# Values of a recurrence projected with tokens on the partitions and shifted through memory and GpSimd, in place of a transpose on TensorE

## The reference, cut to what matters

```python
def rwkv_branch(cur, prev, state0, g, mix, ...):      # prev: the row of the token before
    xs = cur + (prev - cur) * mix                     # token shift
    r, k, v, wd, ad = jnp.split(xs, [512, 1024, 1536, 1600], axis=-1)
    ...
    def step(S, inp):
        sa = jnp.einsum('bhij,bhj->bhi', S, -kk_t)
        S = (S * w_t[:, :, None, :] + sa[..., None] * (kk_t * a_t)[:, :, None, :]
             + v_t[..., None] * k_t[:, :, None, :])
        y = jnp.einsum('bhij,bhj->bhi', S, r_t)
```

## Time and profile before

| | |
|---|---|
| median of 3 runs | 1786.79 us (1780.75 to 1791.63) |
| the profiled execution's own time | 1780.9 us |
| its span | 1779.1 us |
| mean granted clock of TensorE | 0.986 |
| TensorE busy | 1704.3 us, 96% of the span, 21338 matmuls |
| VectorE, ScalarE, GpSimd busy | 827.6, 798.0, 417.3 us |
| token-shift projection | about 554 to 858 us of the span |
| recurrence with gates | about 861 to 1570 us |

### The profile page before, as it was taken

How to read it: one execution, slowest core, us unless ns; L and a number is a source line. 1 busy time by engine, 2 the same in 40 slices (tenths; PEclk the granted TensorE clock), 3 DMA queues, 4 the chain that set the end, 5 groups by cost and what they waited for, 6 DMA issues and landing times. The chain is left out here.

```text
span 1779.1 us, 48548 instructions
## 1 busy us (share of the span) xinstructions
PE 1704.3 (96%) x21338; PEld 1397.0 (79%) x21338; DVE 827.6 (47%) x1198; ACT 798.0 (45%) x1656; POOL 417.3 (23%) x282
## 2 busy tenths in 40 slices
PE   6989999999999999999889999999999999889999
PEld 5768888888887888999667777777777777667787
DVE  4334545445445411223445665565655566643332
ACT  5546665666655322223434444444444444313420
POOL 3322212212210000000214454334444333310000
PEclk9999999999999999999889999999999999989999
DMA  6543353344234412214312112112112113466652
GB/s 227 100 90 64 56 51 69 56 57 80 50 109 173 139 74 86 85 55 151 113 45 66 57 52 79 55 52 71 52 51 78 55 52 120 129 246 232 205 171 92
DMA packets 119139, 170.88 MB, mean 96 GB/s; under 512 B 39569, under 2 KB 78993, under 8 KB 118673
## 3 DMA queue, kind: packets, MB, share of 16 engines
q1 hardware_dynamic: 109568, 153.29, 31.6%
q10 hardware_dynamic: 9360, 14.49, 2.2%
HBM read 113.21 MB, written 55.06 MB: 95 GB/s over the span
## 5 line engine op out<-in xcount | busy, mean ns | idle before, releaser
L653 PE MATMUL a_ps_proj<-a_w_hi,a_x_hi 128*128 128x512 f32 x384 | 156.9, 409 | 0.0
L653 PE MATMUL a_ps_proj<-a_w_hi,a_x_lo 128*128 128x512 f32 x384 | 150.9, 393 | 0.0
L653 PE MATMUL a_ps_proj<-a_w_lo,a_x_hi 128*128 128x512 f32 x384 | 150.6, 392 | 0.0
L1057 DVE SCALAR_TENSOR_TENSOR j_out<-j_ps,j_rest,j_part 128x512 f32<-128x512 f32 (+2 forms) x65 | 41.9, 644 | 213.4 <-ACT j_last_cols L1005 163.3
L563 DVE SCALAR_TENSOR_TENSOR a_stage<-a_ps_s,a_new_bias 128x256 f32<-128x256 f32 x64 | 27.1, 424 | 238.6 <-PE a_ps_s L680 238.6
L2222 PE MATMUL r_ps_gate<-gate_w_hi,gate_x_hi 128*128 128x512 f32 x272 | 115.6, 425 | 4.5 <-PEq L66 3.4
L2222 PE MATMUL r_ps_gate<-gate_w_lo,gate_x_hi 128*128 128x512 f32 x272 | 116.3, 428 | 0.0
L2222 PE MATMUL r_ps_gate<-gate_w_hi,gate_x_lo 128*128 128x512 f32 x272 | 116.2, 427 | 0.0
L1003 ACT ACTIVATE j_part<-j_last_cols,j_shift_in 128x1 f32<-128x1 f32 x65 | 19.2, 295 | 205.8 <-PE j_ps L1082 205.7
L1862 DVE TENSOR_TENSOR r_w_mat<-r_ps_w,consts 128x512 f32<-128x512 f32 x83 | 57.3, 690 | 109.3 <-PE r_ps_w L2106 109.2
L338 POOL TENSOR_TENSOR a_xT<-a_xT,a_row 128x1024 f32<-128x1024 f32 x17 | 40.8, 2402 | 253.2 <-DMA a_row<-scratch_rstd 242.2
(11 more groups left out here) (383 smaller groups left out, 4677.6 us busy)
## 6 DMA issues: line engine op xcount, KB each, us to landing
a_xT<-in_x_T SPq DMA_DIRECT2D x17, 512.0 KB, 3.5
scratch_xT<-a_xT SPq DMA_DIRECT2D x17, 512.0 KB, 2.6
raw<-scratch_xT SPq DMA_DIRECT2D x17, 512.0 KB, 4.0
scratch_gates<-r_gate_out SPq DMA_DIRECT2D x34, 256.0 KB, 2.4
z_gate<-scratch_gates SPq DMA_DIRECT2D x17, 512.0 KB, 4.2
xs<-scratch_xs_T SPq DMA_DIRECT2D x15, 576.0 KB, 4.4
a_x<-in_x_prompt SPq DMA_DIRECT2D x16, 512.0 KB, 12.3
scratch_xs_T<-j_out ACTq DMA_DIRECT2D x39, 192.0 KB, 1.9
```

The source lines that it names most:

```text
L653: mm = nc.tensor.matmul(ps_proj[:], a[n % 2][:, k, :], w[:, k, g * AW:(g + 1) * AW], start=(k == 0 and i == 0), stop=(k == KT - 1 and i == 2))
L1057: last = nc.vector.scalar_tensor_tensor(out=out[j][:, 0:n], in0=ps[j][:, 0:n], scalar=rest[:, c:c + 1], in1=part[j][:, 0:n], op0=ALU.mult, ...
```

## The change

The four v blocks leave the blocks of the projection. In their place come value units, one per tile: x is the stationary operand, the four blocks of v weights (512 columns) the moving one, so the result has tokens on the partitions. The two kinds of unit are listed in `SHIFT_UNITS`: in group 0 all nine blocks and then four values, in the others block and value in turn, then the remaining blocks. The parity of a unit's place in the list chooses its bank and buffers.

The token shift of a value tile goes through memory: ScalarE copies PSUM to `part[j]`, SP stores it to `v_raw`, then loads the same rows one token earlier into `v_prev`, and GpSimd computes `(v_prev - part) * v_share + part` into `out[j]`. SP stores that to `v_tok` in four DMAs, 64 tokens and one half of the heads each. TensorE waits for ScalarE's copy alone behind a value unit. ScalarE may write `part[j]` behind a value unit when GpSimd is done with it; VectorE may write `out[j]` when all earlier stores of that parity have landed. The weights are split in another order (`W_ORDER`, `AHEAD`), two blocks a unit at the end. The last rows of v become an output of their own.

In the recurrence the turning, its two jobs and its two ScalarE copies go; SP loads `v_tok` once whole and once with its halves exchanged.

```diff
+SIZES = (4, 4, 3, 3, 3)
+XS_BLOCKS, V_BLOCKS = (0, 1, 2, 3, 4, 5, 6, 7, 12), (8, 9, 10, 11)
+def shift_units():
+    units = []
+    for g, n in enumerate(SIZES):
+        blocks, values = [(g, c, None) for c in range(XS_TILES)], [(g, None, a) for a in range(n)]
+        if g == 0:
+            units += blocks + values
+        else:
+            for i in range(n):
+                units += [blocks[i], values[i]]
+            units += blocks[n:]
+    return units
+def shift_stores(j, before):
+    return sum((1 if a is None else 4) for q, (g, c, a) in enumerate(SHIFT_UNITS[:before]) if q % 2 == j)
...
+        AHEAD = [[m + 2] for m in range(5)] + [[7, 8], [9, 10], [11, 12]]
+        def part_free(eng, q):
+            if q > 1:
+                if SHIFT_UNITS[q - 2][1] is None:
+                    eng.wait_ge(v_mixed, values(q - 2) + 1)
+                else:
+                    eng.wait_ge(mixed[q % 2], mixes(q - 2) + 1)
...
+            def turn_rows(t, j, i):
+                sp.wait_ge(parted[j], i + 1)
+                sp.dma_start(v_rows(t, 0), part[j][:, 0:AW]).then_inc(v_raw_stored, 16)
+                wait(sp, v_mixed, t)
+                sp.wait_ge(v_set_up, 32)
+                sp.wait_ge(v_raw_stored, 16 * (t + 1))
+                sp.dma_start(v_prev[:], v_rows(t, 1)).then_inc(v_prev_loaded, 16)
+            def store_v(t, j):
+                sp.wait_ge(v_mixed, t + 1)
+                for n in range(2):
+                    tokens = slice(n * CH, (n + 1) * CH)
+                    rows = out[j][tokens, 0:AW].rearrange("l (c g d) -> l c g d", g=2, d=HD)
+                    for g in range(2):
+                        sp.dma_start(io["v_tok"][t, g * CH:(g + 1) * CH, n * PAIRS * HD:(n + 1) * PAIRS * HD].rearrange("l (c d) -> l c d", d=HD),
+                                     rows[:, :, g, :]).then_inc(stored[j], 16)
...
+                    if a is not None:
+                        t = tile_of(g, a)
+                        turn_rows(t, j, i)
+                        if last is not None:
+                            store_v(t - 1, last)
+                        last = j
+                        if a == tiles_of(g) - 1:
+                            store_v(t, j)
...
+                pool.wait_ge(v_prev_loaded, 16 * (t + 1))
+                pool.wait_ge(parted[j], q // 2 + 1)
+                nc.gpsimd.tensor_tensor(v_prev[:], v_prev[:], part[j][:, 0:AW], ALU.subtract).then_inc(v_less, 1)
+                pool.wait_ge(v_less, t + 1)
+                nc.gpsimd.tensor_tensor(v_prev[:], v_prev[:], v_share[:], ALU.mult).then_inc(v_shared, 1)
+                pool.wait_ge(v_shared, t + 1)
+                wait(pool, stored[j], 16 * shift_stores(j, q))
+                nc.gpsimd.tensor_tensor(out[j][:, 0:AW], v_prev[:], part[j][:, 0:AW], ALU.add).then_inc(v_mixed, 1)
...
+                    part_free(act, q)
+                    if a is not None:
+                        nc.scalar.activation(part[j][:, 0:AW], ps[j][:], ACT.Copy).then_inc(parted[j], 1)
...
-                    wait(dve, stored[j], 16 * i)
+                        wait(dve, stored[j], 16 * shift_stores(j, q))
...
-                    wait(pe, mixed[j], i)
+                    if q > 1:
+                        if SHIFT_UNITS[q - 2][1] is None:
+                            pe.wait_ge(parted[j], i)
+                        else:
+                            pe.wait_ge(mixed[j], mixes(q - 2) + 1)
...
+                                x, w = ((x_hi, v_w_hi), (x_hi, v_w_lo), (x_lo, v_w_hi))[e]
+                                mm = nc.tensor.matmul(ps[j][:].rearrange("p (c n) -> p c n", c=len(V_BLOCKS)), x[g % 2][:, k, a, :], w[:, :, k, :],
+                                                      start=(k == 0 and e == 0), stop=(k == KT - 1 and e == 2))
...
-        JOB_ORDER = ((("bonus", -1), ("decay", 0), ("k_tok", -1), ("B0", -1), ("B1", -1), ("v_tok", 0)),
-                     (("iclr", 0), ("b_tok", -1), ("K0", -1), ("K1", -1), ("kk_sum", 0), ("v_swap", 0)))
+        JOB_ORDER = ((("bonus", -1), ("decay", 0), ("k_tok", -1), ("B0", -1), ("B1", -1)),
+                     (("iclr", 0), ("b_tok", -1), ("K0", -1), ("K1", -1), ("kk_sum", 0)))
...
+            def front(t, u, mode):
+                yield 12
+                wait(sp, ready["ps_y"], t - 1)
+                wait(sp, ready["v_bonus"], t - 1)
+                sp.dma_start(v_tok[u][:].rearrange("p m d -> p (m d)"), io["v_tok"][t]).then_inc(v_loaded[u], 16)
+                for g in range(2):
+                    sp.dma_start(v_swap[u][half(g)].rearrange("p m d -> p (m d)"), io["v_tok"][t, half(1 - g), :]).then_inc(v_loaded[u], 16)
...
-                for name, buf in (("v_tok", v_tok), ("v_swap", v_swap), ("k_tok", k_swap), ("b_tok", b_tok)):
+                for name, buf in (("k_tok", k_swap), ("b_tok", b_tok)):
...
-                yield 35.3
-                turn_two(t, "v_tok", xs[u][:, 8:12], "v_swap", xs[u][:, 8:12])
...
+                        v_arrived(pe, t, u)
```

More of the change, by code:

```diff
@@ L874, in prompt_cols, with units, tile_of, mixes @@
             return (SIZES[g] - (g == GROUPS)) * P
-        def blocks(g):
-            for c in range(SHIFT_TILES):
-                i = g * SHIFT_TILES + c
-                yield c, i % 2, i // 2
-        def done(g, j):
-            return ((g + 1) * SHIFT_TILES + 1 - j) // 2
+        W_ORDER = XS_BLOCKS + V_BLOCKS
+        AHEAD = [[m + 2] for m in range(5)] + [[7, 8], [9, 10], [11, 12]]
+        first_unit = [next(q for q, unit in enumerate(SHIFT_UNITS) if unit[0] == g) for g in range(len(SIZES))] + [len(SHIFT_UNITS)]
+        def units(g):
+            for q in range(first_unit[g], first_unit[g + 1]):
+                yield q, q - first_unit[g], SHIFT_UNITS[q][1], SHIFT_UNITS[q][2], q % 2, q // 2
+        def done(g, j):
+            return (first_unit[g + 1] + 1 - j) // 2
+        def tile_of(g, a):
+            return first(g) + a
+        def mixes(q):
+            return sum(unit[1] is not None and i % 2 == q % 2 for i, unit in enumerate(SHIFT_UNITS[:q]))
+        def values(q):
+            return sum(unit[2] is not None for unit in SHIFT_UNITS[:q])
+        def part_free(eng, q):
[4 more added lines that the diff above has]
+                    eng.wait_ge(mixed[q % 2], mixes(q - 2) + 1)
         def by_stream(ap, size):
@@ L966, in split_x, with store @@
                 nc.scalar.activation(x_hi[g % 2][:, k, 0:n, :], xT[:, 0:n, k, :], ACT.Copy).then_inc(x_hi_ready, 1)
-            def store(g, c):
-                n, i = tiles_of(g), g * SHIFT_TILES + c
-                act.wait_ge(mixed[i % 2], i // 2 + 1)
-                act.dma_start(io["xs_T"][c, :, first(g) * P:(first(g) + n) * P], out[i % 2][:, 0:n * P]).then_inc(stored[i % 2], 16)
+            def store(q):
+                g, c, a = SHIFT_UNITS[q]
+                n = tiles_of(g)
+                if c is not None:
+                    act.wait_ge(mixed[q % 2], mixes(q) + 1)
+                    act.dma_start(io["xs_T"][c, :, first(g) * P:(first(g) + n) * P], out[q % 2][:, 0:n * P]).then_inc(stored[q % 2], 16)
             def split_gate_w(i):
@@ L1021, in _ @@
+                    if q > 0:
+                        store(q - 1)
+                    if g < GROUPS and 0 <= m - 3 < KT:
+                        split_x(g + 1, m - 3)
+                    if g == GROUPS and m in (0, 4, 6, 8):
+                        split_gate_w(max(m - 2, 0) // 2)
+                    if g == GROUPS and m == 2:
                         split_gate_x()
-            store(GROUPS, SHIFT_TILES - 1)
+            store(len(SHIFT_UNITS) - 1)
         @block.vector
@@ new lines, in _ @@
+                for q, m, c, a, j, i in units(g):
+                    if g == 0 and m < len(AHEAD):
+                        for b in AHEAD[m]:
+                            split_w(b)
+                    if c is not None:
+                        dve.wait_ge(parted[j], i + 1)
+                        wait(dve, stored[j], 16 * shift_stores(j, q))
+                        b, n = XS_BLOCKS[c], prompt_cols(g)
+                        last = nc.vector.scalar_tensor_tensor(out=out[j][:, 0:n], in0=ps[j][:, 0:n], scalar=rest[:, b:b + 1],
+                                                              in1=part[j][:, 0:n], op0=ALU.mult, op1=ALU.add)
+                        if g == GROUPS:
+                            last = nc.vector.scalar_tensor_tensor(out=by_stream(out[j][:, n:], SL), in0=by_stream(ps[j][:, n:], SL), scalar=rest[:, b:b + 1],
+                                                                  in1=by_stream(part[j][:, 1 + n:], SL + 1)[:, :, 0:SL], op0=ALU.mult, op1=ALU.add)
+                        last.then_inc(mixed[j], 1)
+                    if g < GROUPS and 0 <= m - 3 < KT:
+                        split_x(g + 1, m - 3)
+                    if g == GROUPS and m in (0, 4, 6, 8):
+                        split_gate_w(max(m - 2, 0) // 2)
+                    if g == GROUPS and m == 2:
@@ L1506, in back @@
```

(2 more changed lines are left out.)

212 lines of the change are left out of this document (114 added, 98 removed).

## The result

| | changed kernel | kernel before |
|---|---|---|
| median | 1792.21 us (1789.59 to 1798.82, 11 runs) | 1785.03 us (1780.75 to 1791.63, 11 runs) |
| ratio | 1.0053, interval 1.0036 to 1.0069 | |
| profiled execution, span | 1792.2, 1790.4 us | 1780.9, 1779.1 us |
| mean granted clock | 0.978 | 0.986 |
| projection, first matmul to end of the last | 329.4 us | 304.0 us |

The change costs 0.5%: the projection took 25.4 us more and the recurrence 11.9 us less. The rest is a difference of the phase ahead of both: the projection started 2.2 us earlier in the profile after. That leaves under 1 us open.

A forecast was written before the change was run, and what follows sets the result against it. TensorE was taken to bound both touched stages. Projection +24.7 us (-1.0 + 13.2 + 5.7 + 6.8) and recurrence -12.3 gave +12.4: 1793.3 profiled, 1799 median, own range 1791 to 1810, 8-in-10 range 1776 to 1824.

The forecast's parts named there:

- Part 1: Projection matmuls: regrouped units of 5.44 and 4.16 us gain 1.0 us in all, value units at 512-column speed.
- Part 2: Projection, behind a value unit: copy, store, load, three GpSimd operations and handovers sum to 10.2 us (8.8 to 12.6).
- Part 3: Projection groups 2 to 4: TensorE stalls 4.4 us per group behind the third value's chain and stores, 13.2 in all.
- rival 2: Projection: chain just fits at 9.6 us, stalls 2.6 in three groups, three clock falls; net +2, 1789 us; chance 0.20.
- Part 4: Projection groups 0 and 1: single `v_prev` buffer and backlog give stalls of 3.7 and about 2.0, together 5.7 us.
- Part 5: Projection: granted clock falls to half for 3.4 us behind stalls, costing 1.7 each; four of them 6.8 us.
- Part 6, the boundaries: Recurrence tile boundaries: 0.55 of 1.47 us kept, as the first gate matmul waits for GpSimd's split; fifteen give 8.3.
- Part 6, the warm-up: Recurrence start: 2.3 us gained at the second tile's turning and 1.7 at the first's turning and wait.
- rivals, 1: Projection: GpSimd at 1.6 to 1.7 us beside VectorE's splits, chain 11.0; net +26, 1813 us; chance 0.14.
- Rivals 3: Projection: load lands near 2.1 to 2.3, chain 9.0 or less, clock stays; net -9, 1778 us; chance 0.16.
- 4: Recurrence: the gate's split does not bind, all of the 1.47 returns, -26; net -1, 1786 us; chance 0.06.
- 5: Recurrence waits for loaded values as long as for the turning; projection alone +25, 1812 us; chance 0.04.

The follow-up runs named there:

- Without the memory trip: Changed kernel without the store of raw value rows and the load of the rows before them (values wrong): 1769.0 us, ratio 0.9904 to the kernel before.
- own buffers: Changed kernel with values from group 2 on in x's unused fourth tile, so no block waits for a value chain: 1779.0 us, ratio 0.9964 to before.
- the new order of SyncE's queue: Changed kernel with separate value buffers, a single store per tile, large x load and last value store issued later: 1769.1 us, against 1776.1 without the reordering.
- the kernel with one store: Changed kernel with each value tile's four 64 KB stores made one of 256 KB, loaded in eight pieces: 1785.8 us, ratio 0.9995 to before.
- halving the split: Changed kernel with GpSimd's split of the gate's x in two halves, the first gate matmul waiting for the first alone: 1776.8 us, ratio 0.9966 to before.
- the recurrence alone: Kernel before with only the changed recurrence, loading value tiles that were never turned (results wrong): 1767.4 us, ratio 0.9898 to before.

## Why the prediction was right, point by point

The time, 1792.2 us, lies in the range, 6.8 under the 1799 forecast, and the direction and its cause are those predicted: new waits in the projection that cost more than the turning gave. The forecast change was +12.4 us; the medians give +7.2, the ratio +9.5 (6.4 to 12.3). Part of the agreement is luck: in the shares of the stalls and in the recurrence, errors of opposite sign cancelled.

- **Part 1, arithmetic: right.** Forecast -1.0. Without the memory trip, and with the low clock taken off, the projection is 306.4 - 3.0 = 303.4 us against 304.0. A value unit took 5.44 us in groups 0 and 1 and 5.48 in the others, for the 5.44 assumed, so the strided weights cost next to nothing.
- **Part 2, the chain: right, 7% long.** Forecast 10.2 (0.60, 2.2, 3.0, 4.2 and handovers 0.2), measured 9.5 (0.60, 2.1, 2.8, 4.0).
- **Part 3, groups 2 to 4: the sum right by luck, its shares wrong.** Forecast 4.4 in each of three groups, 13.2. Measured 2.6, 2.5 and 7.6, 12.7. Groups 2 and 3 went as rival 2 had it, since the chain was 0.7 shorter and the four stores took 4.25 and not 4.5. In the last group the forecast priced the sample tile's chain like any other; it took 4.1 and 4.4 us where 2.2 and 3.0 were set.
- "SP holds its loads of x and gate weights, which have one to two units to spare": **wrong**, though it cost little here, as it lay under the longer wait for the stores. With own buffers it came out as 4.5 us in the last group, and the new order of SyncE's queue took 7.0 us off the median.
- **Part 4, groups 0 and 1: the sum near, its shares not.** Forecast 5.7 (3.7 and 2.0), measured 4.7 (1.6, 2.8, 0.3). The first stall, for the stores of group 0's third value, was 1.6. The stall at the end of group 1 was 0.3. The 2.8 at 655 lie between them: TensorE waits there for a ScalarE copy, and that for a chain whose raw store took 7.4 us (640.12 to 647.48) behind the 1.5 MB load. The forecast named that load as a delay of the start, without a price.
- **Part 5, the clock: right in number and sum.** Forecast 6.8. TensorE worked 4.6 us of the long stretch at 0.50 and 3.0 to 3.4 of each of three short ones: half of 14.4 is 7.2. But a gap's length alone does not tell whether the clock falls, as the forecast took it from two rows. In the second profile of the changed kernel a gap of 1.9 us was followed by 3.4 us at 0.50, and in the kernel with one store the clock stayed at 1.00 behind one of 2.4 (the windows right behind the two gaps):

```profile
803.60:807.00 3.40, 3.40 (x13) 3.40 (x12) 1.12 (x3) 0.52 (x1) 0.00 (x0) 0.50 0.19 63
...
656.50:662.00 5.50, 5.50 (x24) 4.56 (x25) 1.77 (x3) 1.54 (x5) 0.55 (x1) 1.00 0.53 191
```

- **Part 6, the boundaries: right.** Forecast 0.55 kept of 1.47 with TensorE waiting about 0.9 at the gate. Measured 0.60 and 0.86; halving the split freed 0.96 more a tile.
- **Part 6, the warm-up: wrong.** Forecast -4.0. Outside the twelve steady tiles the stage is 267.3 us against 264.6, and up to the first gate matmul of the third tile 86.8 against 83.9 (85.8 and 85.3 in the second profiles): nothing won. The wait of 2.85 for VectorE went, and the next in-order wait took its place: 6.0 us at a gate block. The phase also begins 1.0 us later behind its last matmul (gap 4.4 against 3.4), and the clock is low for 34.1 us of this start in place of 13.7 (30.7 and 17.1 in the second profiles), a cost that the forecast left out here; how much of it TensorE paid was not measured.
- **Part 6, what was not forecast: the irregular tiles.** The twelve tiles lost 14.6 us, of which 12 times 0.60 is the price of the turning; 7.4 were longer tiles of the kernel before, of which 5.3 are its five stalls without a releaser and 1.7 the low clock behind one. The forecast read one boundary and multiplied it. In the profiles the two misses cancel, by luck (-11.9 for -12.3); in the medians the recurrence alone gave 18.2, and that is most of what the forecast of the median missed.
- **The sum to the median:** the forecast carried the 5.9 us between profile and median over to the changed kernel. Its own profiled run lay on its median. Another 1.8 us of the 6.8 is the base, 1785.0 over 11 runs where three had given 1786.8. Whether the 5.9 us belonged to the turning, as its irregular tiles suggest, is not shown: over 11 runs each the two kernels spread alike (10.9 and 9.2 us).

Of the rivals, 1 fell: GpSimd's operations met VectorE's splits too seldom to get longer on the whole. A row of the changed kernel (min, median, max in ns), and the longest operation in the timelines of VectorE and GpSimd:

```profile
L1053 POOL TENSOR_TENSOR j_v_prev<-j_v_prev,j_part x17: 1283/1290/1653, 612.0 to 857.3; 128x512 f32<-128x512 f32 x17
...
793.67 0.55 DVE L1145 TENSOR_TENSOR shift_x_lo<-shift_x,shift_x_hi 128x384 fp32r<-128x384 f32 x1
793.72 1.65 POOL L1053 TENSOR_TENSOR j_v_prev<-j_v_prev,j_part 128x512 f32<-128x512 f32 x1 [5.58 <-DMA j_v_prev<-scratch_v_raw]
```

The longest was 1.65 us, and it ran beside a VectorE split of x. The Trainium skill, "GPSIMD Engine Reference", "1. Specifications", has the two contend when VectorE has two SBUF inputs. The trace agrees: of the 51 operations of the chain four took 1.48 to 1.65 us, each beside such a split, and the other 47 took 1.31 at most; one split took 1.62 us in place of 0.55 beside them. But with VectorE busy 71 of 329 us they seldom met, and the price stayed near 1.29. Rivals 3, 4 and 5 fell too: the gaps came, the split did bind, and the recurrence gave its part.

## What to carry to other kernels

A round trip through memory is free only as long as nothing waits for the buffers that it holds: here the 17 us of gaps were waits for buffers that the trip held. Own buffers, 4 KB of room on each partition that was already there, took half of them away, and most of the rest went with one store in place of four and with the order of one queue. Before a DMA is added to a queue that an engine issues in order, write down what stands behind each of its waits, and put a small transfer that a chain waits for ahead of a large one that nobody waits for yet. When work is taken off the bounding engine, look for the next thing it waits for in that very place: the 0.9 us split uncovered by the change was worth 15 us, more than the cost of the whole change.

## What the runs showed of the hardware

- The same 256 KB store took 2.1 to 3.0 us from group 1 on with no large load issued just ahead of it, 3.4 to 4.1 where a load of 512 KB had been issued shortly before, and 7.1 to 8.3 right behind a load of 1.5 MB, though the core's DMA engines were busy only 0.40 of the stage. In the changed kernel they were busy 0.78 from 639.5 to 647.5, but just as busy (0.78 from 640.7 to 643.4) in the kernel with the new order, where the store took 2.75. What was issued ahead of it decided, and no share of DMA tells that.
- The sample tile's 256 KB, cut in eight streams, took 4.1 us out and 4.4 back in place of 2.1 and 2.8.
- The four stores of 64 KB in 256-byte pieces landed in 2.3 us in the median of 68. The Trainium skill, "DMA: Bandwidth & Descriptors", "Anatomy of one DMA", gives by its fit an estimate of 2.15 for that size, nearer than the 2.6 taken from the earlier trace rows; but its fit is of DMAs that GpSimd issues, and these are SyncE's, so that it comes near proves little.
- Turning the values or loading them changes the regularity of the recurrence, beside its speed: twelve tiles took 440.0 and 440.0 us with the loads, 450.0, 454.6 and 459.7 with the turning. The stalls lie inside runs of short matmuls, and each of the 14 ended 1.2 to 1.5 us after a 16 KB packet of the queue named `instruction` had landed.
- A GpSimd operation of 1.29 us took 1.48 to 1.65 beside a VectorE operation on two operands from SBUF, four times in 51; such a VectorE operation took 1.62 us in place of 0.55 once.
- A gap of 1.9 us of TensorE was followed by 3.4 us at a granted clock of 0.50, and one of 2.4 us was not.
